# Second block's first gates around the mixing products of the gated unit, all eight gate blocks kept in place of the gated result

## Chip, cores and metric

One core of one Trainium2 chip runs the whole program. The metric is the device time of one execution in microseconds (us). The kernel before is shown as the median of three executions, and one further execution was profiled.

## What is computed

The reference is a first transformer block (windowed attention, short convolution, 16 experts) followed by a second block. The change lies in the second block alone, in its gated unit and the first of its two gates, for 512 tokens and a width of 1024:

```
h = rms_norm(x, mix_norm_g); proj = h @ w_in
u, v = gelu(proj[..., :768]), gelu(proj[..., 768:1536])
v = rms_norm(v, gmlp_norm_g)                      # over the 768 columns of a token
mixed = einsum('gts,bcsgd->bctgd', tril(w_s), v)  # 4 chunks of 128 tokens, 4 groups
y_a = u * (mixed + b_s)
gates = sigmoid(proj[..., 3840:])                 # 2 x 1024
merged = gates[0] * (y_a @ w_branch_a) + gates[1] * (y_b @ w_branch_b)
```

`y_b` is an attention computed later. The first summand of `merged` is what the kernel forms here and spills to memory until `y_b` is there.

## The kernel before, in words

Every engine has a program of its own, written out by hand in the order in which it runs (functions `tensor`, `scalar`, `vector`, `gpsimd`, `sync`), and the engines meet at semaphores (`wait_ge`, `tick`). TensorE computes in the transposed form: a block is 128 features by 512 tokens, one PSUM bank.

**Weights.** A weight matrix comes in slabs of 256 output columns, in the order in which `piece(...)` lists them. SyncE issues one transfer for a slab into a ring of four places; it waits until the slab four places earlier has been split (L2797 to L2803). A slab is split into a high half (ScalarE copy, `hi`, L1230) and a low half (VectorE subtraction, `lo_half`, L1869). The halves go to one of two pairs of buffers, `wsq0h/wsq0l` and `wsq1h/wsq1l`, by the slab's turn in the list, so a slab can be split only when TensorE has finished the slab two before it. `ahead(key)` on ScalarE and on VectorE splits slab `key`, if that isn't done yet, and the next one. A product takes three matmuls for every 128 rows: high by high, low by high, high by low. So a slab `g0` (256 of the first gate's columns, 8 blocks of rows) is 48 matmuls of 512 columns, and a slab `b0` (256 columns of `w_branch_a`, 6 blocks of rows) is 36.

**Order around the change.** TensorE (L1019 to L1044) runs the products `u2`, then `v2` (three slabs, by tokens), then the mixing products `mix` 0 to 5 (32 calls, which the trace shows as 64 matmuls `ps<-wsT,vg`), then for n = 0 to 3 a slab `g0` n and a slab `b0` n in turn, then the three slabs `av`. Banks are taken in rotation, and a bank is taken again when the reader of its last contents has ticked.

ScalarE (L1618 to L1645) evaluates Gelu on `v2` into `vg`. Then, for each of the four token tiles i, it sums the squares of `vg` (L1630), waits for VectorE's mean and takes the root (L1632). Then it copies `ug` to `yah` six times (high half of `y_a`), and in the gate loop it computes the sigmoid of two blocks of each slab `g0` in `sg`, which is the tile `tb`.

VectorE (L2461 to L2505) prepares the norm's tables for the later attention (`strided`, `r2s`, `cos2`, `sin2`), then goes through the four token tiles: mean, reciprocal (L2474), scaling of `vg` (L2477). Then for each of the six blocks it adds `b_s` (into `tb`), multiplies by `ug` (L2492) and makes the low half `yal` (`left`). In the gate loop it multiplies a gate's product by the row of norms into `sg`, and later the product of `b0` by `sg` into `M2`, the gated result, 8 blocks of 128x512. The trace calls that tile `M`. Afterwards ScalarE issues the spill of the residual stream (`x_spill`) and of `M2` (`m_spill`, L1645), and the first evictions of `av` (ScalarE, L1654) and the splitting of the slab `av` 1 (VectorE, L2509) wait for the spill of `M2` to have landed.

Of the kernel before, what the change touches and what calls it, by code (L numbers as in the profile page):

```python
# [8 lines left out]
T = 512  # L9
# [9 lines left out]
ALU = mybir.AluOpType  # L19
# [85 lines left out]
def emit(nc, a, out, top):  # L105
# [11 lines left out]
    S = {}  # L117
# [230 lines left out]
    def piece(key, w, k0, nk, c0, cols=256, split=True, slot=None, place=None):  # L348
        slab(key, [(0, cols, rows(w, k0, nk, c0, cols))], nk, cols, slot, place, split=split)
# [62 lines left out]
        piece(("v2", n), w_in2, 0, 8, 768 + 256 * n)  # L412
    for n in range(4):
        piece(("g0", n), w_in2, 0, 8, 3840 + 256 * n)
        piece(("b0", n), a["w_branch_a_2"][0], 0, 6, 256 * n)
    for n in range(3):
        piece(("av", n), w_in2, 0, 8, 3072 + 256 * n)
# [50 lines left out]
    def tensor(engine):  # L468
# [59 lines left out]
        def lin(*args, behind=None):  # L528
            for m, k in steps(*args):
                if behind:  # L530
                    behind(m, k)
# [493 lines left out]
        t.then_inc(*S["pe_turn"].tick("ws"))  # L1025
        for n in range(3):
            lin_n(("v2", n), H2h, H2l, [slice(i * P, (i + 1) * P) for i in range(4)], lambda i: [("a_take", (("v2", n), i))])
        for c in range(6):
            b = take(("mix", c), [("v_gmlp", ("add", c))])
            pe.wait_ge(S["v_gmlp"], "wsT")  # L1030
            for i in range(4):
                pe.wait_ge(S["v_gmlp"], ("v", i))
                for p0, n, g in mixes(c):
                    t = mm(ps[p0:p0 + n, b * 512 + i * P:b * 512 + (i + 1) * P], vgv[:, i, c * P + p0:c * P + p0 + n],
                           wsT[:, g * P:(g + 1) * P], True, True)
            t.then_inc(*S["pe_value"].tick(("mix", c)))
        turn["banks"] = [0, 1, 2, 3, 4, 5, 6, 7]
        for n in range(4):
            lin([("g0", n)], H2h, H2l, T, lambda m: [("v_take", (("g0", n), m))])
            lin([("b0", n)], yahv, yalv, T, lambda m: [("v_take", (("b0", n), m))], lambda k: [("v_put", ("ya", k))])  # L1040


# [160 lines left out]
    def scalar(engine):  # L1203
# [4 lines left out]
        def act(o, i, f, bias=None, scale=None, accum=None):  # L1208
            kw = {}
            if bias is not None:  # L1210
                kw["bias"] = bias
            if scale is not None:
                kw["scale"] = scale
            if accum is not None:
                kw["accum_out"] = accum
            return ac_.e.activation(o, i, f, **kw)  # L1216
# [401 lines left out]
        for n in range(3):  # L1618
            ahead(("v2", n))
            for i in range(4):  # L1620
                ac_.wait_ge(S["pe_group"], (("v2", n), i))
                act(vgv[:, i, 256 * n:256 * n + 256], bank(where.get((("v2", n), i), 0), 0, 256), ACT.Gelu,
                    scale=r2[:, i:i + 1]).then_inc(*S["a_take"].tick((("v2", n), i)))
        for i in range(4):
            ac_.wait_ge(S["a_take"], (("v2", 2), i))
            if i:
                ac_.wait_ge(S["a_gmlp"], ("sq", i - 1))
            else:
                ac_.wait_ge(S["pe_norm"], ("f", 7))
            act(tb[:, 0:768], vgv[:, i, :], ACT.Square, accum=rv[:, i:i + 1]).then_inc(*S["a_gmlp"].tick(("sq", i)))  # L1630
            ac_.wait_ge(S["v_gmlp"], ("mean", i))
            act(rv[:, i:i + 1], rv[:, i:i + 1], ACT.Sqrt).then_inc(*S["a_gmlp"].tick(("root", i)))  # L1632
        for c in range(6):
            ac_.wait_ge(S["v_gmlp"], ("mul", c))
            act(yahv[:, c, :], ugv[:, c, :], ACT.Copy).then_inc(*S["a_put"].tick(("ya", c)))
        for n in range(4):
            ahead(("g0", n))
            for m in range(2):
                ac_.wait_ge(S["v_take"], (("g0", n), m))
                act(sg[:, m, :], sg[:, m, :], ACT.Sigmoid).then_inc(*S["a_take"].tick((("g0", n), m)))  # L1640
            ahead(("b0", n))
        ac_.wait_ge(S["v_norm"], ("N", 7))
        load("x_out2", "x", x_d, X[:, :])
# [195 lines left out]
    def vector(engine):  # L1839
# [7 lines left out]
        def ts(o, x, s1, s2, op0, op1):  # L1847
            return v.e.tensor_scalar(o, x, s1, s2, op0, op1)
# [607 lines left out]
        for n in range(3):  # L2456
            ahead(("v2", n))
            for i in range(4):
                next(normed, None)

        s4 = strided.rearrange("p (r j) -> p r j", r=4)  # L2461
        tt(s4, row.rearrange("p (j r) -> p r j", r=4), ident.unsqueeze(1).to_broadcast([P, 4, P]), ALU.mult).then_inc(
# [3 lines left out]
        v.wait_ge(S["v_trig"], "sin")  # L2466
        tt(cos, cos, row, ALU.mult).then_inc(*S["v_trig"].tick("cos2"))
        tt(sin, sin, row, ALU.mult).then_inc(*S["v_trig"].tick("sin2"))
        for i in range(4):
            r = rv[:, i:i + 1]  # L2470
            v.wait_ge(S["a_gmlp"], ("sq", i))
            ts(r, r, 1.0 / 768, 1e-6, ALU.mult, ALU.add).then_inc(*S["v_gmlp"].tick(("mean", i)))
            v.wait_ge(S["a_gmlp"], ("root", i))
            v.e.reciprocal(r, r).then_inc(*S["v_gmlp"].tick(("inv", i)))  # L2474
            v.wait_ge(S["v_gmlp"], ("inv", i))
            v.wait_ge(S["gmlp_in"], "g")
            stt(vgv[:, i, :], vgv[:, i, :], r, gb[:, :], ALU.mult, ALU.mult).then_inc(*S["v_gmlp"].tick(("v", i)))  # L2477
        for c in range(6):
            o = tbv[c % 2]
            b = bank(where.get(("mix", c), 0))  # L2480
            v.wait_ge(S["pe_value"], ("mix", c))
            v.wait_ge(S["v_gmlp"], ("v", 3))
            if c > 1:
                v.wait_ge(S["v_gmlp"], ("mul", c - 2))
            for p0, np_, g in mixes(c):
                r = slice(p0, p0 + np_)
                i = tt(o[r, :].rearrange("p (i t) -> p i t", t=P), b[r, :].rearrange("p (i t) -> p i t", t=P),
                       bs[r, g * P:(g + 1) * P].unsqueeze(1).to_broadcast([np_, 4, P]), ALU.add)
            i.then_inc(*S["v_gmlp"].tick(("add", c)))
            v.wait_ge(S["v_gmlp"], ("add", c))  # L2490
            v.wait_ge(S["a_take"], (("u2", c // 2), c % 2))
            tt(ugv[:, c, :], ugv[:, c, :], o, ALU.mult).then_inc(*S["v_gmlp"].tick(("mul", c)))  # L2492
            left("ya", c, ugv, yahv, yalv)
        for n in range(4):
            ahead(("g0", n))
            for m in range(2):
                v.wait_ge(S["pe_group"], (("g0", n), m))
                v.wait_ge(*((S["v_take"], (("b0", n - 1), m)) if n else (S["v_gmlp"], ("mul", 5))))
                tt(sg[:, m, :], bank(where.get((("g0", n), m), 0)), row, ALU.mult).then_inc(*S["v_take"].tick((("g0", n), m)))
            ahead(("b0", n))  # L2500
            for m in range(2):
                v.wait_ge(S["pe_group"], (("b0", n), m))
                v.wait_ge(S["a_take"], (("g0", n), m))
                tt(M2v[:, 2 * n + m, :], bank(where.get((("b0", n), m), 0)), sg[:, m, :], ALU.mult).then_inc(
                    *S["v_take"].tick((("b0", n), m)))  # L2505

# [389 lines left out]
```

## Time and profile before

| what | us |
|---|---|
| median of 3 executions (lowest, highest) | 2092.52 (2092.1, 2094.34) |
| the profiled execution, its own time | 2092.72 |
| span of its records | 2090.9 |
| TensorE busy with matmuls | 1918.9, 92% of the span, 9773 matmuls |
| VectorE, ScalarE, GpSimd busy | 957.6, 657.1, 88.2 |
| mean granted clock of TensorE | 0.962 of full speed |

In the rows below a matmul is a record of PE, a weight load one of PEld; DVE is VectorE, ACT is ScalarE, SPq the queue of transfers of SyncE. The last columns of a row of the timeline, in brackets, are the time that the engine stood idle before it and what ended that. Matmuls are pipelined: a record of a 128x512 matmul is 0.39 us long, and the next starts 0.23 us after it did. A row of the windows view gives a stretch (start:end), its length, the busy time of the engine with the number of its records, the granted clock of TensorE as a share of 2.4 GHz (0.50 is 1.2 GHz), the share of the time in which the transfer engines were busy, and GB/s. The profile covers one execution, the slowest core (here the only one).

### The profile page before, as it was taken

To read this page: it belongs to the slowest core of one execution; us is meant where nothing else is said; L and a number is where in the kernel's file an instruction comes from. 1 tells how busy PE (TensorE), PEld (TensorE's weight loads), DVE (VectorE), ACT (ScalarE), POOL (GpSimd) and SP (SyncE) were. 2 spreads that over 40 slices of the span, in tenths; PEclk is the share of its full clock that TensorE was granted. 3 is DMA by queue.
4 is the path that set the end of the run, shared out by engine and by line. 5 is a ranking of instruction groups with operands and counts; after the bars stand their busy time and mean duration, and the time that the engine had idled before them with its cause. 6 is when DMAs were issued, how large, how long until landed. Compare 5 with 4: busy or idle time off the path is not lost. (4 is left out here: it accounts for less than half of the span.)

```text
span 2090.9 us, 23513 instructions
## 1 busy us (share of the span) xinstructions
PE 1918.9 (92%) x9773; PEld 1397.6 (67%) x9779; DVE 957.6 (46%) x1611; ACT 657.1 (31%) x1137; POOL 88.2 (4%) x70
## 2 busy tenths in 40 slices
PE   6899999899999699999998898998889889999998
PEld 4677777678878434343432487897677677888877
DVE  4787767752552322221311345314454536636642
ACT  4444444342232311020200233223545323223232
POOL 0110000000000000000000000002030200000000
PEclk9899999999999799999999998999999999999999
DMA  9323232243342599999999731341111412243221
GB/s 317 103 80 112 92 111 91 81 161 101 107 176 106 190 410 409 409 409 409 409 409 409 274 109 56 106 155 53 48 61 41 142 60 91 66 136 101 68 83 41
DMA packets 201117, 355.16 MB, mean 170 GB/s; under 512 B 7122, under 2 KB 148530, under 8 KB 200242
## 3 DMA queue, kind: packets, MB, share of 16 engines
q1 hardware_dynamic: 197264, 338.85, 45.0%
q10 hardware_dynamic: 3458, 14.50, 1.9%
q8 instruction: 77, 1.26, 0.2%
q0 software_dynamic: 288, 0.30, 0.1%
q14 instruction: 30, 0.25, 0.0%
HBM read 345.53 MB, written 8.39 MB: 169 GB/s over the span
## 5 line engine op out<-in xcount | busy, mean ns | idle before, releaser
L475 PE MATMUL ps<-H,wsq0h 128*128 128x512 f32 x704 | 223.7, 400 | 12.3 <-DVE wsq0l L1845 10.3
L475 PE MATMUL ps<-H,wsp0h 128*128 128x512 f32 x576 | 189.3, 408 | 13.9 <-ACT H L1216 8.0
L475 PE MATMUL ps<-H,wsq1h 128*128 128x512 f32 x544 | 173.9, 402 | 10.5 <-DVE wsq1l L1845 10.5
L475 PE MATMUL ps<-rx,XE 128*64 128x512 f32 x752 | 177.4, 601 | 4.8 <-DMA rx<-in_w_exp_up 3.1
L475 PEld LDWEIGHTS ps<-H,wsq0h 128*128 128x128 f32 x704 | 134.2, 193 | 41.6 <-issue 12.6
L475 PE MATMUL ps<-H,wsq0l 128*128 128x512 f32 x352 | 139.5, 396 | 0.0
L475 PEld LDWEIGHTS ps<-H,wsp0h 128*128 128x128 f32 x576 | 107.1, 194 | 37.9 <-issue 10.4
L1845 DVE TENSOR_TENSOR wsq0l<-ring,wsq0h 128x1024 fp32r<-128x1024 f32 (+2 forms) x72 | 81.4, 1165 | 110.7 <-ACT wsq0h L1216 110.7
L475 PE MATMUL ps<-H,wsp1h 128*128 128x512 f32 x336 | 111.9, 415 | 20.9 <-DVE wsp1l L1845 20.9
L475 PEld LDWEIGHTS ps<-H,wsq1h 128*128 128x128 f32 x544 | 104.1, 193 | 34.1 <-issue 12.8
L475 PE MATMUL ps<-H,wsp0l 128*128 128x512 f32 x288 | 115.2, 400 | 0.0
L475 PEld LDWEIGHTS ps<-rx,XE 128*64 128x64 f32 x752 | 49.0, 136 | 97.2 <-issue 82.0
L475 PE MATMUL ps<-H,wsq1l 128*128 128x512 f32 x272 | 107.8, 396 | 0.0
L475 PE MATMUL ps<-rx,hT 128*64 128x512 f32 x368 | 98.7, 605 | 7.3 <-DMA rx<-in_w_exp_down 7.1
L1854 DVE SCALAR_TENSOR_TENSOR X<-ps,modT,X 128x512 f32<-128x512 f32 x72 | 53.9, 750 | 105.6 <-PE ps L475 105.6
L1845 DVE TENSOR_TENSOR wsq1l<-ring,wsq1h 128x1024 fp32r<-128x1024 f32 (+3 forms) x72 | 76.9, 1103 | 51.6 <-ACT wsq1h L1216 51.2
L1216 ACT ACTIVATE tb<-ps 128x512 f32<-128x512 f32 (+1 forms) x44 | 26.0, 592 | 197.8 <-PE ps L475 197.8
L475 PEld LDWEIGHTS ps<-H,wsp1h 128*128 128x128 f32 x336 | 61.2, 195 | 34.1 <-issue 18.6
L1216 ACT ACTIVATE wsq0h<-ring 128x1024 fp32r<-128x1024 f32 (+2 forms) x72 | 66.8, 975 | 45.7 <-PE ps L475 45.6
L1845 DVE TENSOR_TENSOR tb<-ps,tb 128x512 f32<-128x512 f32 x40 | 27.5, 689 | 112.3 <-PE ps L475 112.1
L475 PE MATMUL ps<-KR,wsp1h 128*128 128x512 f32 x256 | 78.8, 389 | 0.0
L475 PEld LDWEIGHTS ps<-H,wsq0l 128*128 128x128 f32 x352 | 67.7, 192 | 14.7
(361 smaller groups left out, 3636.5 us busy)
## 6 DMA issues: line engine op xcount, KB each, us to landing
rx<-in_w_exp_gate SPq DMA_DIRECT2D x49, 1024.0 KB, 18.3
rx<-in_w_exp_down SPq DMA_DIRECT2D x46, 1024.0 KB, 18.5
rx<-in_w_exp_up SPq DMA_DIRECT2D x45, 1024.0 KB, 18.6
ring<-in_w_in SPq DMA_DIRECT2D x39, 1024.0 KB, 5.3
ring<-in_w_up SPq DMA_DIRECT2D x20, 1024.0 KB, 5.1
ring<-in_w_exp_up SPq DMA_DIRECT2D x19, 1024.0 KB, 18.8
ring<-in_w_mod SPq DMA_DIRECT2D x18, 1024.0 KB, 6.0
ring<-in_w_exp_down SPq DMA_DIRECT2D x18, 1024.0 KB, 18.6
```

The costliest lines, as they stand in the source:

```text
L475: return pe.e.matmul(o, l, r, start=start, stop=stop, skip_group_check=True)
L1216: return ac_.e.activation(o, i, f, **kw)
L1845: return v.e.tensor_tensor(o, x, y, op)
L1854: return v.e.scalar_tensor_tensor(o, x, s, y, op0, op1)
```

## The change

The slabs are listed, and so fetched and split, in the order `g0` 0 to 3, then `b0` 0 to 3. TensorE runs `g0` 0 and 1 before the mixing products, `g0` 2 and 3 behind them, then the four slabs `b0`. The rotation of the banks is set to 0 to 7 before `g0` 0. The gates of all eight blocks are kept in `M2`, first the scaled product, then its sigmoid in place, then the product of `b0` by it in place. `sg` is no longer used here. The mean, root and reciprocal of the four token tiles are computed in one instruction each, behind all four sums of squares. On VectorE the tables for the later attention stand behind gate 0, and the low half of a block of `y_a` is made one block later.

```diff
--- before.py
+++ after.py
@@ -412,6 +412,7 @@
         piece(("v2", n), w_in2, 0, 8, 768 + 256 * n)
     for n in range(4):
         piece(("g0", n), w_in2, 0, 8, 3840 + 256 * n)
+    for n in range(4):
         piece(("b0", n), a["w_branch_a_2"][0], 0, 6, 256 * n)
     for n in range(3):
         piece(("av", n), w_in2, 0, 8, 3072 + 256 * n)
@@ -1025,6 +1026,13 @@
         t.then_inc(*S["pe_turn"].tick("ws"))
         for n in range(3):
             lin_n(("v2", n), H2h, H2l, [slice(i * P, (i + 1) * P) for i in range(4)], lambda i: [("a_take", (("v2", n), i))])
+        turn["banks"], turn["n"] = [0, 1, 2, 3, 4, 5, 6, 7], 0
+
+        def gate0(n):
+            lin([("g0", n)], H2h, H2l, T, lambda m: [("v_take", (("g0", n), m))])
+
+        gate0(0)
+        gate0(1)
         for c in range(6):
             b = take(("mix", c), [("v_gmlp", ("add", c))])
             pe.wait_ge(S["v_gmlp"], "wsT")
@@ -1034,9 +1042,9 @@
                     t = mm(ps[p0:p0 + n, b * 512 + i * P:b * 512 + (i + 1) * P], vgv[:, i, c * P + p0:c * P + p0 + n],
                            wsT[:, g * P:(g + 1) * P], True, True)
             t.then_inc(*S["pe_value"].tick(("mix", c)))
-        turn["banks"] = [0, 1, 2, 3, 4, 5, 6, 7]
+        gate0(2)
+        gate0(3)
         for n in range(4):
-            lin([("g0", n)], H2h, H2l, T, lambda m: [("v_take", (("g0", n), m))])
             lin([("b0", n)], yahv, yalv, T, lambda m: [("v_take", (("b0", n), m))], lambda k: [("v_put", ("ya", k))])
 
 
@@ -1621,6 +1629,7 @@
                 ac_.wait_ge(S["pe_group"], (("v2", n), i))
                 act(vgv[:, i, 256 * n:256 * n + 256], bank(where.get((("v2", n), i), 0), 0, 256), ACT.Gelu,
                     scale=r2[:, i:i + 1]).then_inc(*S["a_take"].tick((("v2", n), i)))
+        ahead(("g0", 0))
         for i in range(4):
             ac_.wait_ge(S["a_take"], (("v2", 2), i))
             if i:
@@ -1628,16 +1637,19 @@
             else:
                 ac_.wait_ge(S["pe_norm"], ("f", 7))
             act(tb[:, 0:768], vgv[:, i, :], ACT.Square, accum=rv[:, i:i + 1]).then_inc(*S["a_gmlp"].tick(("sq", i)))
-            ac_.wait_ge(S["v_gmlp"], ("mean", i))
-            act(rv[:, i:i + 1], rv[:, i:i + 1], ACT.Sqrt).then_inc(*S["a_gmlp"].tick(("root", i)))
-        for c in range(6):
-            ac_.wait_ge(S["v_gmlp"], ("mul", c))
-            act(yahv[:, c, :], ugv[:, c, :], ACT.Copy).then_inc(*S["a_put"].tick(("ya", c)))
+        ac_.wait_ge(S["v_gmlp"], "mean")
+        act(rv, rv, ACT.Sqrt).then_inc(*S["a_gmlp"].tick("root"))
         for n in range(4):
             ahead(("g0", n))
+            if n == 2:
+                for c in range(6):
+                    ac_.wait_ge(S["v_gmlp"], ("mul", c))
+                    act(yahv[:, c, :], ugv[:, c, :], ACT.Copy).then_inc(*S["a_put"].tick(("ya", c)))
             for m in range(2):
+                o = M2v[:, 2 * n + m, :]
                 ac_.wait_ge(S["v_take"], (("g0", n), m))
-                act(sg[:, m, :], sg[:, m, :], ACT.Sigmoid).then_inc(*S["a_take"].tick((("g0", n), m)))
+                act(o, o, ACT.Sigmoid).then_inc(*S["a_take"].tick((("g0", n), m)))
+        for n in range(4):
             ahead(("b0", n))
         ac_.wait_ge(S["v_norm"], ("N", 7))
         load("x_out2", "x", x_d, X[:, :])
@@ -2457,6 +2469,23 @@
             ahead(("v2", n))
             for i in range(4):
                 next(normed, None)
+        ahead(("g0", 0))
+        v.wait_ge(S["a_gmlp"], ("sq", 3))
+        ts(rv, rv, 1.0 / 768, 1e-6, ALU.mult, ALU.add).then_inc(*S["v_gmlp"].tick("mean"))
+        v.wait_ge(S["a_gmlp"], "root")
+        v.e.reciprocal(rv, rv).then_inc(*S["v_gmlp"].tick("inv"))
+        v.wait_ge(S["v_gmlp"], "inv")
+        v.wait_ge(S["gmlp_in"], "g")
+        for i in range(4):
+            stt(vgv[:, i, :], vgv[:, i, :], rv[:, i:i + 1], gb[:, :], ALU.mult, ALU.mult).then_inc(*S["v_gmlp"].tick(("v", i)))
+
+        def gate0(n):
+            for m in range(2):
+                v.wait_ge(S["pe_group"], (("g0", n), m))
+                tt(M2v[:, 2 * n + m, :], bank(where.get((("g0", n), m), 0)), row, ALU.mult).then_inc(
+                    *S["v_take"].tick((("g0", n), m)))
+
+        gate0(0)
 
         s4 = strided.rearrange("p (r j) -> p r j", r=4)
         tt(s4, row.rearrange("p (j r) -> p r j", r=4), ident.unsqueeze(1).to_broadcast([P, 4, P]), ALU.mult).then_inc(
@@ -2466,15 +2495,8 @@
         v.wait_ge(S["v_trig"], "sin")
         tt(cos, cos, row, ALU.mult).then_inc(*S["v_trig"].tick("cos2"))
         tt(sin, sin, row, ALU.mult).then_inc(*S["v_trig"].tick("sin2"))
-        for i in range(4):
-            r = rv[:, i:i + 1]
-            v.wait_ge(S["a_gmlp"], ("sq", i))
-            ts(r, r, 1.0 / 768, 1e-6, ALU.mult, ALU.add).then_inc(*S["v_gmlp"].tick(("mean", i)))
-            v.wait_ge(S["a_gmlp"], ("root", i))
-            v.e.reciprocal(r, r).then_inc(*S["v_gmlp"].tick(("inv", i)))
-            v.wait_ge(S["v_gmlp"], ("inv", i))
-            v.wait_ge(S["gmlp_in"], "g")
-            stt(vgv[:, i, :], vgv[:, i, :], r, gb[:, :], ALU.mult, ALU.mult).then_inc(*S["v_gmlp"].tick(("v", i)))
+        ahead(("g0", 1))
+        gate0(1)
         for c in range(6):
             o = tbv[c % 2]
             b = bank(where.get(("mix", c), 0))
@@ -2490,19 +2512,21 @@
             v.wait_ge(S["v_gmlp"], ("add", c))
             v.wait_ge(S["a_take"], (("u2", c // 2), c % 2))
             tt(ugv[:, c, :], ugv[:, c, :], o, ALU.mult).then_inc(*S["v_gmlp"].tick(("mul", c)))
-            left("ya", c, ugv, yahv, yalv)
+            if c == 1:
+                ahead(("g0", 2))
+            if c:
+                left("ya", c - 1, ugv, yahv, yalv)
+        left("ya", 5, ugv, yahv, yalv)
+        for n in (2, 3):
+            ahead(("g0", n))
+            gate0(n)
         for n in range(4):
-            ahead(("g0", n))
-            for m in range(2):
-                v.wait_ge(S["pe_group"], (("g0", n), m))
-                v.wait_ge(*((S["v_take"], (("b0", n - 1), m)) if n else (S["v_gmlp"], ("mul", 5))))
-                tt(sg[:, m, :], bank(where.get((("g0", n), m), 0)), row, ALU.mult).then_inc(*S["v_take"].tick((("g0", n), m)))
             ahead(("b0", n))
             for m in range(2):
+                o = M2v[:, 2 * n + m, :]
                 v.wait_ge(S["pe_group"], (("b0", n), m))
                 v.wait_ge(S["a_take"], (("g0", n), m))
-                tt(M2v[:, 2 * n + m, :], bank(where.get((("b0", n), m), 0)), sg[:, m, :], ALU.mult).then_inc(
-                    *S["v_take"].tick((("b0", n), m)))
+                tt(o, bank(where.get((("b0", n), m), 0)), o, ALU.mult).then_inc(*S["v_take"].tick((("b0", n), m)))
```

## Rows read from the trace of the kernel before

**Rows 1.** Windows view, PE alone, from the last `v2` product to `av`

```profile
1267.60:1364.20 96.60, 87.58 (x401) 0.93 0.30 95
```

**Rows 2.** Waits of TensorE in the same stretch: total us, times, longest

```profile
PE ps L475 <- DVE small L1848: 5.7, 3, 4.2
PE ps L475 <- issue: 2.6, 1, 2.6
```

**Rows 3.** Timeline of TensorE, where it changes from one product to the next

```profile
1267.31 0.28 PE L475 MATMUL ps<-wsq1l,H 128*128 128x256 f32 x1
...
1276.39 7.33 PE L475 MATMUL ps<-wsT,vg 128*128 128x128 f32 x58 [0.76 <-DVE vg L1854]
1283.48 0.71 PE L475 MATMUL ps<-H,wsq0h 128*128 128x512 f32 x2
...
1297.23 0.75 PE L475 MATMUL ps<-yah,wsq1h 128*128 128x512 f32 x1 [2.59 <-issue]
...
1307.07 0.62 PE L475 MATMUL ps<-H,wsq0h 128*128 128x512 f32 x2
...
1317.95 0.39 PE L475 MATMUL ps<-yah,wsq1h 128*128 128x512 f32 x1
...
1326.11 0.62 PE L475 MATMUL ps<-H,wsq0h 128*128 128x512 f32 x2
...
1364.19 0.40 PE L475 MATMUL ps<-wsq0h,H 128*128 128x256 f32 x2
```

**Rows 4.** Windows view, weight loads (PEld) of the mixing products alone

```profile
1276.38:1279.70 3.32, 2.76 (x22) 0.50 0.00 0
1279.70:1280.50 0.80, 0.80 (x7) 0.70 0.00 0
1280.50:1283.44 2.94, 2.65 (x33) 1.00 0.00 0
```

**Rows 5.** Windows view, PE alone: start of `b0` 0, and the later gates

```profile
1297.20:1300.70 3.50, 3.47 (x8) 0.51 0.65 208
1310.00:1364.20 54.20, 54.20 (x241) 1.00 0.42 136
```

**Rows 6.** Timeline of ScalarE: sum of squares, table load, split, sigmoid

```profile
1268.00 0.83 ACT L1216 ACTIVATE tb<-vg 128x768 f32<-128x768 f32 x1
...
1268.94 1.28 ACT L1216 ACT_TABLE_LOAD   x1
...
1298.89 1.99 ACT L1216 ACTIVATE wsq0h<-ring 128x1024 fp32r<-128x1024 f32 x2
...
1313.43 0.63 ACT L1216 ACTIVATE tb<-tb 128x512 f32<-128x512 f32 x1 [4.52 <-DVE tb L1845]
```

**Rows 7.** Timeline of VectorE: a table, scaling of `vg`, an addition, splits, a gated block

```profile
1260.49 1.09 DVE L1845 TENSOR_TENSOR hT<-tb,cst 128x512 f32<-128x512 f32 x1
...
1275.32 1.02 DVE L1854 SCALAR_TENSOR_TENSOR vg<-vg,small,gb 128x768 f32<-128x768 f32 x1
...
1279.94 1.39 DVE L1845 TENSOR_TENSOR tb<-ps,bs 64x512 f32<-64x512 f32 x2
...
1295.30 1.83 DVE L1845 TENSOR_TENSOR wsq1l<-ring,wsq1h 128x768 fp32r<-128x768 f32 x2
...
1299.97 2.36 DVE L1845 TENSOR_TENSOR wsq0l<-ring,wsq0h 128x1024 fp32r<-128x1024 f32 x2 [1.64 <-ACT wsq0h L1216]
...
1303.19 0.69 DVE L1845 TENSOR_TENSOR M<-ps,tb 128x512 f32<-128x512 f32 x1 [0.86 <-PE ps L475]
```

**Rows 8.** Timeline: issue of the spill of `M2`, and what waits for it

```profile
1365.11 0.33 ACTq L1239 DMA_DIRECT2D m_spill<-M  x1
...
1372.56 2.35 DVE L1845 TENSOR_TENSOR wsq1l<-ring,wsq1h 128x1024 fp32r<-128x1024 f32 x2
...
1375.70 0.63 PE L475 MATMUL ps<-wsq1h,H 128*128 128x256 f32 x2
```

**Rows 9.** Transfers by line: issues, KB each, median us from issue to landing

```profile
m_spill<-M ACTq DMA_DIRECT2D x1, 2048.0 KB, 7.3
```

## The prediction

> **What bounds the kernel now.** TensorE is busy for 92% of the span, so I first looked for what it still waits for in the stretch that the change touches. From the last product of `v2` to the first of `av` it has 96.6 us, is busy for 87.6 of them and runs at a mean clock of 0.93 [rows 1]. So there are two kinds of loss: about 9 us of idle time, and time in which the array is busy at half speed. From 1310 us on the same loop of gates runs without a gap at clock 1.00 [rows 5]. The losses therefore lie ahead of that.
>
> The waits name them [rows 2]: 5.7 us for the norm of `v` (mean, root, reciprocal, scaling), in three pieces of which the longest is 4.2 us, and 2.6 us put down to "issue". The timeline shows where [rows 3]. Behind the last `v2` product TensorE stands idle, does the first 6 of the 64 mixing matmuls in bursts, one for each token tile that comes ready, then the remaining 58 from 1276.39 us on; `g0` 0 starts at 1283.48. The "issue" wait stands ahead of `b0` 0, and VectorE shows its real cause: the low half of that slab is split from 1295.30 for 1.83 us [rows 7], ended at 1297.13, and TensorE starts at 1297.23. That split stands behind the six blocks of `y_a` in ScalarE's program and in VectorE's. After each of these gaps the clock is at half: 0.50 until 1279.7 and 0.51 from 1297.2 to 1300.7 [rows 4, 5].
>
> **What the stretch costs without waits.** A clean `g0` slab takes 1317.95 - 1307.07 = 10.88 us, a clean `b0` slab 1326.11 - 1317.95 = 8.16 us [rows 3]. Both kinds come four times before and after the change, 76.2 us together. The mixing products are 64 matmuls. At full clock 33 of their weight loads take 2.94 us, or 0.089 us each, which makes 5.7 us; at half clock 22 take 3.32 us, or 0.151 each, 9.7 us [rows 4]. After the change they follow 21.8 us of dense products, and stand ahead of more, so I take 5.7 and keep 9.7 as the upper end. The lower end is 5.2 us, if only the 58 matmuls of one run are scaled by their clock (3.32 x 0.50 + 0.80 x 0.70 + 2.94) and the first six are nearly free. The Trainium skill ("TensorE: Matmul & The Clock Gate", Back-to-back issue gap) has about 81 ns for each pair of weight load and 128-column matmul in a stream. By that figure the products would take 5.2 us and the saving be half a microsecond larger; the row is of the same instructions, so it decides.
>
> Before, the stretch from the end of `v2` (the next product could have started about 0.12 us behind 1267.31) to `av` is 1364.19 - 1267.43 = 96.8 us. After, it is 76.2 + 5.7 = 81.9 us, plus some 0.1 us at each of two changes between forms, so 82.1. The difference is **14.7 us**. The same sum from the losses: 1283.48 - 1267.43 - 5.7 = 10.3 us ahead of `g0` 0, 2.6 us of wait, 1.7 us of half clock in `b0` 0 (1307.07 - 1297.23 - 8.16), 0.1 at the start of `g0` 0.
>
> **Is each step in time?** The forecast needs every split and every reader to be done before TensorE asks. I set the new programs against a dense TensorE: `g0` 0 from 1267.5, `g0` 1 from 1278.4, mixing from 1289.3, `g0` 2 from 1295.1, `g0` 3 from 1306, `b0` 0 from 1316.9, then every 8.16 us, `av` from 1349.5. A split of a `g0` slab is 2.0 us on ScalarE and 2.36 on VectorE, which starts when the first half is there and so ends some 1.4 us later [rows 6, 7]. A `b0` slab has three quarters of the columns: 1.5 and 1.83 us, ending 1.1 us later.
> - Transfers: the same eight slabs in another order, each issued when the slab four places earlier is split. `b0` 1 to 3 are issued behind the splits of `g0` 1 to 3, so from 1271.5 to 1296.3, and wanted from 1325 on: over 35 us ahead. SyncE's queue holds nothing else.
> - `g0` 1: its buffer is free with the last `v2` product. Split by 1271.5, wanted at 1278.4.
> - The norm: ScalarE's four sums of squares now start at 1270.1, behind that split, at about 1.07 us each (the engine was free 0.94 us behind the start of one, and each waits for the one before), then the table load of 1.28 and the root, 1275.9; VectorE scales four tiles at 1.02 us [rows 6, 7], so `v` is ready at 1280.4. Wanted at 1289.3: 9 us of cover. Batching the means removes three small instructions of each kind from both engines; none is on TensorE's path any more, so I cost it at nothing. Were `g0` 0 and 1 not there to cover it, this chain would be longer than before, 12.8 us.
> - Gate 0 (two multiplications of 0.69 us) and the attention tables (four instructions, none above the 1.09 of the first, so 4.4 at most) follow on VectorE, ending by 1286.2. ScalarE loads the sigmoid's table (1.28), computes two sigmoids of 0.63, then splits `g0` 2 at 1282.4 to 1284.4, VectorE by 1288.6 [rows 6, 7]. Wanted at 1295.1.
> - `y_a`: six blocks are each an addition (0.69, or 1.39 in two of them), a multiplication and a low half, 0.69 each, so 13.8 us, with the split of `g0` 3 (2.36) between [rows 7]. From 1290.1 that is 1307. Split of `g0` 3 by 1296.3, wanted at 1306. Behind that stand two multiplications of gate 2 (1.4), the last sigmoid (0.63), then the split of `b0` 0 (1.5 + 1.1): 1311.6, say 1312.5 with hand-overs, wanted at 1316.9. This 4.4 us is the thinnest cover in the new order. The gates 2 wait in their banks meanwhile, from which nobody is kept: `g0` 2 and 3 use banks 2 to 5, `b0` 0 banks 6 and 7.
> - `b0` 1 to 3 and `av` 0: the buffer is free 8.16 us ahead of use, splitting takes some 3.4 at most.
> - Banks: each of the mixing products' banks 4 to 7, 0, 1 was read long before. Gates in `M2` have the size of those in `tb`.
> - `av` 1: VectorE begins its low half at 1372.56, when the spill of `M2` (issued at 1365.11, 7.3 us) has landed, ends at 1374.91, and TensorE wants it at 1375.70 [rows 8, 9]. All of that hangs on the end of `b0` 3 and moves with it. The ring transfer behind the split of `av` 0 and the spill of X are released 8.16 us ahead of that end or more, so they don't come closer to it than before, and the margin of 0.8 us should hold or grow.
> Behind `av` the programs are unchanged and each wait is relative to TensorE, so the whole difference should reach the end.
>
> **The number.** 14.7 from the profiled execution's 2092.7 gives 2078.0. The median of the runs is 0.2 us below that execution, which I leave aside.
>
> **Rivals.**
> - *A late hand-over inside the new order* (0.11). ScalarE or VectorE has more in its queue than I counted, and TensorE waits ahead of `b0` 0 or a mixing product. Against it are covers of 4 to 10 us. For it: the old order lost just such a wait. A gap like the old one costs 2.6 + 1.7 = 4.3 us, so 2082.3.
> - *The mixing products don't keep the clock* (0.05). They are short, and half of them use 64 columns of weights. The Trainium skill (same page, HAM oscillation, second failure mode) says that small idle times between groups of matmuls can make the clock swing. Rows bear on it: at half clock, they raised it to 1.00 within one unbroken run, 1276.39 to 1280.5 [rows 3, 4]. If they lost it all the same they would take 9.7 us and `g0` 2 would pay about 1.7, together 5.7: 2083.7.
> - *It doesn't do what it says, or the time is given back* (0.03), say at the waits of the attention behind `av`: 2092.
> - *Slower, by the spill of M2* (0.02). Its place is the landing that the low half of `av` 1 and the first evictions wait for. X's spill, two ring loads of 1 MB and the 2 MB of `M2` now fall into a denser stretch. Delays count one for one beyond 8.1 us from issue to landing; it decides the sign only beyond 8.1 + 14.7 = 22.8 us, three times what it took. At 28 us it would give 2098.
> - *As forecast* (0.79).
>
> **Range and chances.** The forecast's own spread is 5.2 to 7 us for the mixing products, a few tenths at changes of form, and a microsecond either way for where later gaps meet a change of the clock: 2075.5 to 2080.5. To reach the first rival the upper end goes to 2082.8. What a measurement can tell from no change is 0.2%, about 4 us. Faster by more than that is the forecast and the first two rivals, 0.95; the same 0.03; slower 0.02.
>
> **What would show it.** In the changed profile the waits of TensorE from the last `v2` product to the first `av` product should be near nothing, that stretch some 82 us long at clock 1.00, mixing products dense within 6 us, and the low half of `b0` 0 ended some microseconds before its first product. The three waits for `small` and `vg` should be gone. After `av` both traces should agree shifted by the same amount. It would be wrong if a wait for `wsq0l`, `yal` or `vg` stands in the new stretch, if the clock there is under 0.97, or if the shift shrinks behind `av`.

## The result, and the profile after

The changed kernel takes 2080.44 us (median of four executions, 2077.56 to 2081.55), the one before 2092.6 (2092.1 to 2094.34). The ratio is 0.9938, with a 95% interval of 0.9921 to 0.9956. That is 12.2 us less; forecast were 2078.0 us and 14.7 us less. In two later measurements the same kernel came to 2076.73 and 2078.03 us beside 2093.44 for the one before, 16.7 and 15.4 us less. The 14.7 lie within that spread, and the question was what makes it, and whether a steady part hides in it.

The profiled execution took 2081.55 us, its span is 2079.8. First the stretch between the last `v2` product and `av`, in the windows view (columns as in [rows 1]):

```profile
1269.50:1351.80 82.30, 82.30 (x403) 1.00 0.34 111
```

The view of waits lists none in it; before there were 87.6 busy microseconds in 96.6, at a clock of 0.93 [rows 1, 2]. The timeline of TensorE, beside [rows 3]:

```profile
1269.38 0.28 PE L476 MATMUL ps<-wsq1l,H 128*128 128x256 f32 x1
1269.50 0.63 PE L476 MATMUL ps<-H,wsq0h 128*128 128x512 f32 x2
...
1280.41 0.62 PE L476 MATMUL ps<-H,wsq1h 128*128 128x512 f32 x2
...
1291.29 6.17 PE L476 MATMUL ps<-wsT,vg 128*128 128x128 f32 x64
1297.22 0.71 PE L476 MATMUL ps<-H,wsq0h 128*128 128x512 f32 x2
...
1319.09 0.39 PE L476 MATMUL ps<-yah,wsq0h 128*128 128x512 f32 x1
...
1351.73 0.40 PE L476 MATMUL ps<-wsq0h,H 128*128 128x256 f32 x2
```

All 64 mixing matmuls run without a break, in 1297.22 - 1291.29 = 5.93 us. From the last `v2` product to `av` it is 1351.73 - 1269.38 = 82.35 us, before 96.88: **14.53 us less**, where 14.7 were forecast. ScalarE and VectorE, beside [rows 6, 7], and the wait for the spill, beside [rows 8, 9]:

```profile
1270.08 2.00 ACT L1224 ACTIVATE wsq1h<-ring 128x1024 fp32r<-128x1024 f32 x2
1271.97 0.83 ACT L1224 ACTIVATE tb<-vg 128x768 f32<-128x768 f32 x1
...
1276.00 1.28 ACT L1224 ACT_TABLE_LOAD   x1
1277.29 0.21 ACT L1224 ACTIVATE small<-small 128x4 f32<-128x4 f32 x1
```

```profile
1277.74 3.81 DVE L1866 SCALAR_TENSOR_TENSOR vg<-vg,small,gb 128x768 f32<-128x768 f32 x4
...
1291.49 0.69 DVE L1857 TENSOR_TENSOR M<-ps,tb 128x512 f32<-128x512 f32 x1 [2.95 <-PE ps L476]
1292.38 0.69 DVE L1857 TENSOR_TENSOR tb<-ps,bs 128x512 f32<-128x512 f32 x1 [0.20 <-PE ps L476]
...
1306.67 1.48 DVE L1857 TENSOR_TENSOR yal<-ug,yah 128x512 fp32r<-128x512 f32 x2
...
1310.78 1.83 DVE L1857 TENSOR_TENSOR wsq0l<-ring,wsq0h 128x768 fp32r<-128x768 f32 x2 [1.43 <-ACT wsq0h L1224]
...
1359.59 2.35 DVE L1857 TENSOR_TENSOR wsq1l<-ring,wsq1h 128x1024 fp32r<-128x1024 f32 x2
```

```profile
m_spill<-M ACTq DMA_DIRECT2D x1, 2048.0 KB, 6.8
```

`vg` is ready at 1281.55, 9.7 us ahead of the mixing products; `y_a` at 1308.15 and the slab of `b0` 0 at 1312.61, 6.5 us ahead of their use. The slab `av` 1 is ready at 1361.94 and wanted 1.3 us later (0.8 before), since the spill of `M2` landed in 6.8 us and not 7.3.

The rest of the span, cut at the same products in both kernels: the last of `v2`, the first of `av`, the first of `k2h` (the scores of the second attention), the last of `va` (its values), and the first of `hfh` (the last projection).

| part, us | before | after | difference |
|---|---|---|---|
| start to last `v2` | 1267.31 | 1269.38 | +2.1 |
| last `v2` to first `av` | 96.88 | 82.35 | -14.5 |
| first `av` to first `k2h` | 106.4 | 106.5 | +0.1 |
| first `k2h` to last `va` | 148.3 | 152.1 | +3.8 |
| last `va` to first `hfh` | 209.4 | 209.6 | +0.2 |
| first `hfh` to end | 262.6 | 259.9 | -2.7 |

Two parts that the change doesn't touch became longer, and one became shorter. The first has the same instructions in both. The windows view of its beginning, before and then after, shows little other than the clock, 0.91 and then 0.89:

```profile
0.00:120.00 120.00, 91.58 (x580) 0.91 0.59 192
```

```profile
0.00:120.00 120.00, 91.50 (x571) 0.89 0.57 186
```

### The profile page after: what moved, and what is told of

The parts are those of the page before. It is cut to its first block and busy times, and to the rows that moved or that the text cites. A ratio compares the mean times of both kernels' runs of the same rounds, so it can differ in the third digit from the quotient of the medians.

```text
span 2079.8 us, 23499 instructions
## 1 busy us (share of the span) xinstructions
PE 1918.0 (92%) x9773; PEld 1398.0 (67%) x9779; DVE 956.0 (46%) x1605; ACT 656.9 (32%) x1134; POOL 87.6 (4%) x70
## 5 line engine op out<-in xcount | busy, mean ns | idle before, releaser
L476 PE MATMUL ps<-H,wsq0h 128*128 128x512 f32 x640 | 205.5, 403 | 10.8 <-DVE wsq0l L1857 8.8
L476 PE MATMUL ps<-H,wsq1h 128*128 128x512 f32 x608 | 194.9, 403 | 10.5 <-DVE wsq1l L1857 10.5
L476 PEld LDWEIGHTS ps<-H,wsq0h 128*128 128x128 f32 x640 | 123.2, 195 | 37.9 <-issue 11.1
L476 PEld LDWEIGHTS ps<-H,wsq1h 128*128 128x128 f32 x608 | 117.0, 194 | 36.9 <-issue 12.8
L476 PE MATMUL ps<-H,wsq0l 128*128 128x512 f32 x320 | 127.7, 399 | 0.0
L476 PE MATMUL ps<-H,wsq1l 128*128 128x512 f32 x304 | 121.0, 398 | 0.0
L476 PEld LDWEIGHTS ps<-rx,XE 128*64 128x64 f32 x752 | 49.0, 136 | 96.6 <-issue 82.4
L1224 ACT ACTIVATE wsq1h<-ring 128x1024 fp32r<-128x1024 f32 (+3 forms) x72 | 64.2, 939 | 36.8 <-PE ps L476 27.3
L476 PEld LDWEIGHTS ps<-rx,hT 128*64 128x64 f32 x368 | 33.6, 139 | 57.8 <-issue 42.6
```

The source lines that it names most:

```text
L476: return pe.e.matmul(o, l, r, start=start, stop=stop, skip_group_check=True)
```

## The experiments

**The changed kernel again, twice.** Nothing was edited (`e0_after_again`, `e11_after_third`).

> The changed kernel once more. In the stretch between the last v2 product and the first av product it saved 14.5 us in the profile, but its profiled execution is only 11.2 us shorter than that of before, and its median 12.2 us. Theory A (the clock is granted at points that don't move with the kernel, so each short wait elsewhere costs more or less half-clock time by chance): the stretch is 82.3 us again within 0.2, while the points outside it where the clock is at half differ from those of the last profile, and the attention stage behind av (first product of k2h to the last of pT) is not again 3.8 us longer than the 148 us it took before the change. The median lies between 2077 and 2082, and single runs differ by 2 us or more. Theory B (the new order lastingly costs something behind av): the attention stage is again longer by 3 us or more, at the same waits.

> The changed kernel a third time, as the partner of the next two. The sum of what was found so far is 14.5 us in the stretch of the gates and 2.7 us by the banks near the end, 17.2 us: the median should be 15 to 19 us below that of before, the stretch 82.35 us, first hfh to the end 259.9 us. If it is again 12 us, a loss behind av that comes and goes is still missing from the account.

The medians were 2076.73 us (ratio 0.9919, 0.9905 to 0.9932) and 2078.03 us (0.9922, 0.9908 to 0.9935). The stretch was 82.35 us both times, and first `hfh` to the end 259.9 both times. The attention stage took 149.0 and 148.5 us, so the 3.8 us of the first profile did not come back: theory B is out. A long attention stage doesn't belong to the new order either, for it took 152.6 us in `e1_tiles` and 152.4 us in `e2_batched`, which has the old order. The second median lies 0.3 us under its forecast of 2077 to 2082 us, the third 15.4 us below the kernel before (forecast 15 to 19). Span and mean granted clock, from the view of the cores, of the first profile, of the second and of the third:

```profile
core 0: 2079.8 us, clock 0.962
```

```profile
core 0: 2073.2 us, clock 0.965
```

```profile
core 0: 2070.2 us, clock 0.967
```

One program gives spans 9.6 us apart. Taken as time at half clock, 2 x (1 - clock) x span, it is 158 us in the first and 137 in the third: 21 us less of it go with a span 9.6 us shorter. So time at half clock outside the gates is enough to account for the spread; why it falls at different places from one execution to the next was not shown, only that it does so with nothing edited.

**The batching.** It was undone in the changed kernel (`e1_tiles`), and put alone into the kernel before (`e2_batched`).

```diff
--- after.py
+++ e1_tiles.py      (VectorE, the calls of then_inc left out; ScalarE alike)
-        v.wait_ge(S["a_gmlp"], ("sq", 3))
-        ts(rv, rv, 1.0 / 768, 1e-6, ALU.mult, ALU.add)
-        v.wait_ge(S["a_gmlp"], "root")
-        v.e.reciprocal(rv, rv)
+        for i in range(4):
+            r = rv[:, i:i + 1]
+            v.wait_ge(S["a_gmlp"], ("sq", i))
+            ts(r, r, 1.0 / 768, 1e-6, ALU.mult, ALU.add)
+            v.wait_ge(S["a_gmlp"], ("root", i))
+            v.e.reciprocal(r, r)
...
```

> The changed kernel with the mean, root and reciprocal of vg token tile by token tile again, as before the change. My theory (9 us of cover in front of the mixing products make the batching worth nothing): the same as the changed kernel, within 1 us, no wait of TensorE in the stretch, which is 82.3 us. Rival (the batching carries part of the gain): 2 us or more slower than the changed kernel, with a wait for vg or small.

Median 2077.07 us (ratio 0.9917, 0.9903 to 0.993) beside 2076.73 for the changed kernel in the same measurement; the stretch 82.35 us, no wait in it. Under the cover of `g0` 0 and 1 the batching is worth nothing.

> The kernel before with the batching alone: order of products unchanged. My theory (uncovered, the batched chain hands over the first tile later and the last one some 1.5 us later): 0.5 to 2.5 us slower than before, TensorE's first wait behind v2 grows from 4.2 us to about 8, and the three short ones are gone. Rival (fewer small steps between ScalarE and VectorE are a gain by themselves): 1 us or more faster than before.

```profile
PE ps L475 <- DVE vg L1854: 7.3, 1, 7.3
PE ps L475 <- issue: 1.4, 1, 1.4
```

```profile
1273.90:1284.90 11.00, 10.64 (x63) 0.58 0.00 0
1284.90:1297.40 12.50, 11.20 (x51) 1.00 0.00 1
1297.40:1305.70 8.30, 8.24 (x36) 1.00 0.53 159
```

Median 2095.59 us, ratio 1.0009 (1.0000 to 1.0018): at most a slight loss, about where I expected it. In the views (waits, then windows) the first wait has grown to 7.3 us, as expected, and the mixing products behind it take 11.0 us at a clock of 0.58. The last tile of `vg` is ready 10.3 us behind the start of the last `v2` product, before 9.0. But the stretch as a whole is 96.56 us, 0.3 shorter than before: `b0` 0 waits 1.4 us in place of 2.6, and keeps its clock. What the first wait loses, the second and its clock give back.

**Cover ahead and behind.** One gate ahead of the mixing products and three behind (`e3_one_ahead`); two ahead and none (`e4_none_behind`) or one (`e6_one_behind`) between them and `b0` 0. The programs of ScalarE and VectorE were put in the same order, and in the last two the list of slabs as well. Each ran once (2080.28, 2082.34 and 2077.04 us). Single executions of one program lie several microseconds apart, so only the stretch is compared.

```diff
--- after.py
+++ e3_one_ahead.py        (TensorE)
         gate0(0)
-        gate0(1)
         for c in range(6):
...
+        gate0(1)
         gate0(2)
--- after.py
+++ e4_none_behind.py      (TensorE; e6: g0 2, b0 0, g0 3, b0 1, b0 2, b0 3)
-        gate0(2)
-        gate0(3)
-        for n in range(4):
-            lin([("b0", n)], ...)
+        for which, n in (("b0", 0), ("g0", 2), ("b0", 1), ("g0", 3), ("b0", 2), ("b0", 3)):
+            if which == "g0":
+                gate0(n)
+            else:
+                lin([("b0", n)], ...)
```

> The changed kernel with one gate product, g0 0, ahead of the mixing products in place of two, and three behind. In the changed kernel the last token tile of vg is ready 12.2 us after the last v2 product starts, the first 9.4 us after. One g0 slab covers 11.0 us of it. My theory (cover is all that counts): TensorE waits about 1.2 us for vg, and the stretch from the last v2 product to the first av product, 82.35 us in each profile of the changed kernel, becomes 83 to 84.5 us. Rival (two gates are needed because VectorE must also be through gate 0 and the tables before the mixing products): 3 us or more longer.

```profile
PE ps L476 <- DVE vg L1866: 0.4, 1, 0.4
```

The stretch was 82.99 us: a wait of 0.4 us (not 1.2), 0.6 us in all. One slab ahead does nearly as well as two. The rival with VectorE's gate 0, for which 3 us or more were expected, falls.

> The changed kernel with g0 0 and 1 ahead of the mixing products, but b0 0 directly behind them, then g0 2, b0 1, g0 3, b0 2, b0 3 (slabs listed in that order). In the changed kernel the last low half of y_a is ready 38.8 us after the last v2 product starts; here TensorE would want it at about 29. My theory: b0 0 waits for yal, 7 to 8 us in all, and a half-clock stretch of 1 to 2 us may come with it: the stretch of 82.35 us becomes 89.5 to 92.5 us. So the gates behind the mixing products are worth half of the gain or more. Rival (the gates ahead of the mixing products bring it all): under 85 us.

```profile
PE ps L477 <- DVE yal L1858: 4.8, 5, 1.4
```

```profile
1295.00:1306.00 11.00, 6.20 (x18) 0.77 0.23 71
1306.00:1312.00 6.00, 6.00 (x24) 0.86 0.01 3
```

The stretch was 90.86 us, within the forecast 89.5 to 92.5: `b0` 0 waits for five of the six low halves in turn, and runs partly at half clock. The waits come to 4.8 us, not the 7 to 8 that I expected; the other 3.7 of the 8.5 us are matmuls that take longer, in part at half clock. Of the gain of 14.5 us, 8.5 need something behind the mixing products.

> The changed kernel with only g0 2 between the mixing products and b0 0; then g0 3, b0 1, b0 2, b0 3. My theory: one slab of 10.9 us covers the chain of y_a just as well, since it is ready at 38.8 us and b0 0 is wanted at 38.8 us, its last row of weights some 3 us later: the stretch is 82.35 us, at most 0.5 more. Rival (both gates behind are needed): over 83 us, with a wait for yal or for a split.

82.35 us, no wait. So one of the two gate products behind is margin, and with three behind the second one ahead is worth 0.6 us. One ahead and one behind together were not run.

**The clock's share.** Matmuls that nobody reads were put into the waits of the kernel before; they leave every result as it is. In `e5_before_filled` 16 stand behind `v2` and 18 ahead of `b0` 0; in `e10_before_filled_all` three more stand between the bursts of the first mixing products, and 15 ahead of `b0` 0.

```diff
--- before.py
+++ e10_before_filled_all.py
+        hold(0, [])
+        for k in range(16):
+            mm(bank(0), H2h[:, k % 8, 0:P], H2h[:, 0, :], True, True)
         for c in range(6):
...
             for i in range(4):
+                if c == 0 and i:
+                    for k in range(3):
+                        mm(bank(0), H2h[:, k, 0:P], H2h[:, 0, :], True, True)
                 pe.wait_ge(S["v_gmlp"], ("v", i))
...
             lin([("g0", n)], ...)
+            if n == 0:
+                hold(7, [])
+                for k in range(15):
+                    mm(bank(7), H2h[:, k % 8, 0:P], H2h[:, 0, :], True, True)
```

> The kernel before with matmuls that nobody reads put into two waits of TensorE: 16 of 512 columns behind v2 (3.6 us, into bank 0) and 18 behind g0 0 (4.1 us, into bank 7). No result changes. My theory (1.7 us of the gain in b0 0, and 2 us or more in the mixing products, were half clock behind an idle stretch): the clock is 1.00 in b0 0, which takes 8.2 us in place of 9.8, and the mixing products end earlier, but b0 0 still starts when VectorE has split its slab, at most 0.7 us earlier; together 1.5 to 2.5 us faster than before. Rival (only the waits themselves cost): the same as before within 0.5 us or slower by what the added matmuls overrun.

The mixing products as a whole, four parts of that stretch, and `b0` 0:

```profile
1271.30:1283.00 11.70, 9.04 (x63) 0.71 0.00 1
...
1271.30:1273.00 1.70, 0.65 (x3) 0.98 0.00 0
1273.00:1275.00 2.00, 1.15 (x4) 0.50 0.00 0
1276.00:1278.00 2.00, 2.00 (x16) 0.50 0.00 0
1280.00:1283.00 3.00, 3.00 (x34) 1.00 0.02 5
...
1298.10:1306.20 8.10, 8.10 (x37) 1.00 0.64 209
```

`b0` 0 ran at full clock in 8.16 us, as expected (9.84 before). The mixing products did not get theirs: their last 58 took 7.1 us as before. The clock was still 0.98 at the first tile, fell to 0.50 while TensorE did two matmuls for each tile with waits between, and came back within the run of 58. And 18 were too many; `b0` 0 started 1.4 us late. The stretch was 96.57 us, the median 2092.95 us (ratio 0.9999, 0.9991 to 1.0008), short of the 1.5 to 2.5 us that I expected.

> The kernel before with matmuls that nobody reads in the waits of the gated unit, as in e5, but also three between the bursts of the first mixing products, and 15 in place of 18 ahead of b0 0. Theory (the mixing products lost their clock for the whole sparse stretch, not just for the first gap): the 58 mixing matmuls that end the stretch take 5.2 to 5.6 us in place of 7.1, g0 0 starts some 1.8 us earlier, but b0 0 starts at most 0.7 us earlier, since VectorE's chain of y_a sets it; it then runs at full clock. The stretch of 96.9 us becomes 94 to 95.5. Rival (full clock there brings its whole 3.4 us): under 93.7.

```profile
1275.08 5.61 PE L475 MATMUL ps<-wsT,vg 128*128 128x128 f32 x58 [0.37 <-DVE vg L1864]
```

```profile
1295.62 0.47 PE L475 MATMUL ps<-yah,wsq1h 128*128 128x512 f32 x1 [0.63 <-issue]
```

```profile
1266.80:1363.00 96.20, 93.94 (x455) 77.04 (x454) 45.91 (x64) 29.90 (x45) 0.00 (x0) 1.00 0.33 102
```

Here the whole stretch ran at clock 1.00 in the one execution that was made (2092.01 us), and was 95.03 us, within the forecast 94 to 95.5. The last 58 mixing matmuls took 5.4 us (before 7.1) and `b0` 0 took 8.3 (9.8), 3.3 us less together, and yet the stretch is only 1.85 us shorter. That is what full clock is worth in the old order. `b0` 0 starts 29.6 us behind the last `v2` product, before 29.9: VectorE's chain sets that start, and the earlier end of the mixing products moved it by only 0.3 us. The other 12.7 us of the gain are waits, which stand in this kernel too, in part filled with matmuls that nobody reads; the new order took them away.

**The banks near the end.** The rotation of PSUM banks was set on by three ahead of `wo2` in the kernel before (`e8_before_banks`), so that the last product `val` lies in bank 3, where the changed kernel has it; and by four in the changed kernel (`e9_after_banks`), so that it lies in bank 0, where the kernel before has it. Every product from `wo2` on moves with it. The next product, the first of the last projection's second half, always takes bank 0.

```diff
--- before.py
+++ e8_before_banks.py       (e9, on after.py: += 4)
         turn["banks"] = [0, 1, 2, 3, 4, 5, 6]
+        turn["n"] += 3
         for _ in wide(("wo2", 0), ...)
```

> The kernel before with the rotation of the PSUM banks set on by three ahead of the product wo2, nothing else. From the first product of the second half of the last layer's down projection's inputs (first hfh) to the end of the span all kernels with the old order have 262.6 us (3 profiles), all with the new order 259.9 (3 profiles). In the old one TensorE waits 2.1 us near 2010 us for VectorE to read the bank 0 that the last product val left full, and runs at half clock behind it; in the new one that product lies in bank 3, since fewer banks were taken in the rotation. My theory (the change shifted the rotation and so took this wait away, 2.7 us that I did not forecast): first hfh to the end is 259.9 us here too, and the kernel is 2 to 3.5 us faster than before. Rival (it is due to the earlier end of the gates): 262.6 us, no change in time.

> The changed kernel with the rotation of the banks set on by four ahead of wo2, so that the last product val lies in bank 0 again as before the change. Theory (the 2.7 us near the end are due to the bank alone): first hfh to the end is 262.6 us again, with the wait of 2.1 us for VectorE, and the kernel is 2 to 4 us slower than the changed one. Rival (the order of the gates has a part in it): 259.9 us.

The waits of TensorE from the first `hfh` product to the end, those that differ: before, then `e8_before_banks`, then `e9_after_banks`.

```profile
PE ps L475 <- DVE ac L1845: 2.1, 1, 2.1
PE ps L475 <- DVE wsq0l L1845: 1.0, 1, 1.0
```

```profile
PE ps L475 <- DVE wsq0l L1846: 2.0, 2, 1.0
```

```profile
PE ps L476 <- DVE ac L1858: 2.1, 1, 2.1
```

The wait comes and goes with the rotation alone, in both orders. `e8_before_banks` has 259.9 us from first `hfh` to the end, and is faster than the kernel before: 2088.98 us, ratio 0.9976 (0.9966 to 0.9986). That is 5.0 us, of which the end has 2.7.

More of it lies in the part ahead, from the last `va` to the first `hfh`, which takes 206.3 us (209.4 before). The waits of TensorE there, those that differ, before and then in `e8_before_banks`:

```profile
PE ps L475 <- DVE wsq1l L1845: 5.2, 2, 3.8
PE ps L475 <- ACT tb L1216: 2.8, 1, 2.8
...
PE ps L475 <- DVE X L1845: 1.2, 1, 1.2
```

```profile
PE ps L475 <- DVE wsq1l L1846: 3.8, 1, 3.8
PE ps L475 <- DVE X L1846: 2.8, 1, 2.8
```

One wait of 2.8 us at the start of `wo2` stands in place of three (1.4, 2.8 and 1.2 us). `e9_after_banks` shows the same change, with a wait of 4.3 us, and has 207.7 us for that part, where the three profiles of the changed kernel have 208.9 to 209.6. The twelve profiles other than these two have 207.9 to 211.2 us there, so the saving is clear for `e8_before_banks` and only likely for `e9_after_banks`.

At the end `e9_after_banks` has 261.1 us, not the 262.6 that I expected: the wait is back (2.1 in place of 1.0 us), but the clock did not fall behind it in this execution.

```profile
1990.00:2020.00 30.00, 27.88 (x129) 1.00 0.30 97
```

Its median of 2077.10 us (0.992, 0.9907 to 0.9934) can't be told from the 2078.03 of the changed kernel, where 2 to 4 us more were expected; the 1.2 us that the end loses are about what the part ahead has less. So near the end the bank costs 1.2 us in every profile that has it, and 1.5 us more, with half clock, in four of the five (262.6 or 262.7 us in all four of the old order).

**Filling waits in the changed kernel.** Thirteen matmuls that nobody reads, ahead of the first scores of each half of the second attention (`e7_after_filled`).

```diff
--- after.py
+++ e7_after_filled.py
             for r in range(4):
+                if r == 0:
+                    hold(6, [])
+                    for k in range(13):
+                        mm(bank(6), H2h[:, k % 8, 0:P], H2h[:, 0, :], True, True)
                 scores2(jj, r)
```

> The changed kernel with 13 matmuls of 512 columns that nobody reads (2.9 us, into bank 6) ahead of the first scores of each of the two halves of the second attention, where TensorE waits 3.0 us for the keys and often runs at half clock for some microseconds behind. No result changes. Theory (these waits cost clock as well as time, and the clock outside the gates is what makes runs differ): the scores start at full clock, the kernel is 1 to 4 us faster than the changed one, first k2h to last va takes 145 to 149 us. Rival (the clock there falls for the short, sparse products of the scores themselves): within 1 us of the changed kernel.

The 21.4 us from the end of the products ahead of that point, in `e7_after_filled` and then in the third profile of the changed kernel:

```profile
1451.60:1473.00 21.40, 20.09 (x95) 1.00 0.15 49
1473.00:1500.00 27.00, 24.37 (x142) 0.87 0.13 39
```

```profile
1449.30:1470.70 21.40, 18.15 (x82) 0.92 0.16 50
1470.70:1498.00 27.30, 23.08 (x143) 0.94 0.12 39
```

The clock holds behind the filled wait, and falls some microseconds later instead. The attention stage took 148.2 us (148.5), the median was 2076.53 us (ratio 0.9915, 0.9902 to 0.9929) beside 2078.03: 1.5 us less, which the two intervals don't tell from nothing, so that neither the theory (1 to 4 us) nor the rival (within 1 us) is shown. No version here beats the changed kernel beyond doubt.

## Why the prediction was right, and where it was not

- **The number.** 2080.44 us lies in the range, 2.4 us above the forecast. The later medians are 1.3 us below it and on it. The total was 12.2, 16.7 and 15.4 us less in the three measurements, and two things move it that I did not have: 2.7 us more near the end, and a clock that moves single executions by several microseconds. That the total came so close to 14.7 is partly luck.
- **The stretch.** 14.53 us for 14.7. The mixing products took 5.93 us for 5.7, the slabs 10.88 and 8.16 us as taken from [rows 3]. Their price by the Trainium skill ("TensorE: Matmul & The Clock Gate", Back-to-back issue gap), an estimate of 5.2 us, was further off.
- **The covers.** All held. `vg` was ready 12.2 us behind the start of the last `v2` product (forecast 13.1), `y_a` 38.8 (39.7), the slab of `b0` 0 43.2 (45.2). My figures were each a little late, since I added whole records, and an instruction starts some 0.1 us before the record of the one ahead of it ends: four scalings took 3.81 us and not 4.08. For the slab I had also added 0.9 us of hand-overs. The tables took 3.0 us and not the 4.4 that I allowed, but that gained nothing: VectorE then stood idle for 2.95 us until TensorE had the second block of gate 1. `e3`, `e4` and `e6` show where the covers end: shortening the one ahead to a single slab costs 0.6 us, taking everything behind away costs 8.5.
- **The batching** was rightly costed at nothing (`e1`). That the chain would be longer without cover was right as well (7.3 us of wait in `e2`), but that this makes the old order slower was not shown: the stretch stayed as long.
- **The step that failed** is the sentence that behind `av` the programs are unchanged and the whole difference reaches the end. The instructions are the same, but the banks that they use are not: the change takes the gates' banks in another place of the rotation and sets its count back to 0 (the first block of `wo2` lies in bank 6, before in bank 3), and so shortened a wait 650 us later from 2.1 to 1.0 us. It went in the kernel's favour, by 1.2 to 2.7 us, and I had no case for it.
- **The losses.** I summed 1.7 us of half clock in `b0` 0 and some in the mixing products as if each counted. The sum is right, since the difference of the ends doesn't ask for the parts; but `e10` shows that with the old order full clock alone returns 1.85 us, because a matmul that ends sooner waits longer for `y_a`.
- **The rivals.** None came. The first had no wait to show. For the second the clock stayed at 1.00 through the mixing products; I had priced them at 9.7 us at half clock, and `e2` shows 11.0 at 0.58, so that price was too low. In the kernel before, too, they are sparse at first and then dense, and `e5` shows the clock fall from 0.98 to 0.50 while they are sparse and rise to 1.00 in the dense run. The Trainium skill ("TensorE: Matmul & The Clock Gate", A second HAM failure mode: psum-queue depth-cycling) describes a clock that swings between its two levels where TensorE idles briefly and often between groups of matmuls; these rows agree, with one fall and one rise. The spill of `M2` landed sooner, not later.

## What to carry to other kernels

When a chain of small steps on ScalarE and VectorE stands between two products, look for independent products to put in front of it and behind it; the length of the chain against the length of one slab says how many are needed (here one ahead with three behind cost 0.6 us, two ahead with one behind nothing). Sum the new order end to end rather than adding up the losses of the old one: a clock or a wait that is restored ahead of another wait is swallowed by it. And where buffers are taken in rotation, a change in the number taken moves every later conflict: compare the bank of each product before and after, not just the instructions.

## What the runs showed that I had not expected

- Three profiles of one program have spans from 2070.2 to 2079.8 us, with a mean granted clock from 0.967 to 0.962. All waits of TensorE within the changed stretch are absent in each, and that stretch is 82.35 us in all three. A stretch can thus be compared to a few hundredths of a microsecond where the whole is uncertain by several.
- An idle time of 2.6 us ahead of `b0` 0 was followed by half clock [rows 3, 5], one of 1.4 us in `e2` was not, and one of 2.1 us near the end was in four of the five profiles that have it, but not in that of `e9`.
- Matmuls put into a wait held the clock at 1.00 behind it in `e10` and in `b0` 0 of `e5`, and for some microseconds in `e7`, but not ahead of the sparse first mixing products in `e5`. They brought 1.85 us at most (`e10`): there another wait came a little later, and in `e7` the clock fell later instead.
- With the order of products as it was, another rotation from `wo2` on made the kernel before 5.0 us faster (`e8`). The changed kernel has the same banks from `wo2` on, but other ones in the product `bb` ahead of it, and it has only the part of this gain near the end. An order and a rotation that have both were not run.
